# A two-block-plus-one transformer kernel: score matmuls a block ahead, maxima ahead of the scaling, weighted values ahead of the transposes, constant products at the head of attention units

## The chip, the cores and the metric

One core of one Trainium2 chip runs the whole program in one launch. The metric is the device time in microseconds (us). The tensor engine (TensorE, PE in the rows), the vector engine (VectorE, DVE), the scalar engine (ScalarE, ACT), GpSimd (POOL) and the DMA queues (SP among them) each run their own instruction list in order and meet by semaphores.

## The reference

Three layers follow each other on 1024 tokens of width 1024. The change concerns their attention parts:

```python
# layer 1: 8 heads of 64, chunks of 64 queries see their own and the 8 chunks before
scores = einsum('bcqhd,bckhd->bhcqk', qc, kb) * Dh ** -0.5 + bias   # masked: -1e30
probs = softmax(scores, axis=-1)
out = einsum('bhcqk,bckhd->bcqhd', probs, vb)
# layer 2: 8 query heads on 2 key heads, window of 128 to both sides, with a sink
mx = maximum(s.max(-1), sk); e = exp(s - mx)
prob = e / (e.sum(-1) + exp(sk - mx))
# layer 3: attention of 8 heads to a neighbourhood of 8 rows x 16 columns of a grid,
# relative bias, gated by silu(z); beside it a depthwise convolution of 31 taps
```

Everything else (projections, spatial gating, mLSTM scan, feed-forward parts, norms) is computed by both versions in the same way.

## The kernel before

Activations lie feature-major. Every weight block (128 x 1024) is split by GpSimd into a high and a low part (lines 2046 and 2060), and TensorE makes three products per tile (`product`, `block_part`: line 389, 407). These fill most of the time.

Attention is done for two heads at a time (a "unit"): four units in layer 1 (buffers `band_...`, keys of 128, 256, 384, 512 and then four times 640 for the eight blocks of 128 queries), four in layer 2 (`local_...`, called with `joint=True`, 256 or 384 keys) and four in layer 3 (`near_...`, 512 or 576 keys). In a unit the eight query blocks p = 0 to 7 go through the same steps:

- S(p), `score`: the scores of both heads on TensorE, into the two accumulators `acc[0]` and `acc[1]`, one a head (line 709; in layer 2 both heads share one accumulator, line 697). It first waits until both accumulators are free.
- `take_scores(p)` on VectorE (line 813, in layer 2 line 777) adds the bias, writes the negated scores and their minimum, and frees the accumulators.
- `exponential(p)` on ScalarE (line 854, 846), with the sum of the row.
- `norm_probs(p)` on VectorE: reciprocal of the sum (line 823, 789) and scaling (line 826, 793).
- T(p), `turn_probs`: TensorE transposes the probabilities in tiles of 128 (line 720) into three PSUM banks `turned`, and `copy_turned(p)` on ScalarE copies them to SBUF (lines 864, 870).
- W(p), `weigh_values`: TensorE multiplies them by the values (line 744).

The order on each engine is written out by hand. TensorE runs, for n = 0 to 9: S(n), T(n-1), W(n-2) (layer 2: S(n+1), T(n-1), W(n-2)). At n = 8 and 9 it also runs pieces of the next weight block (three tiles ahead of T(7), one ahead of W(7)), which cover the last waits. VectorE runs `norm_probs(p-1)` and then `take_scores(p)`; in layer 2 the other way round. ScalarE runs `exponential(n)` and then `copy_turned(n-1)`, in all layers and in both versions.

In layer 3 the scores are exponentiated in place (`scores=None`). VectorE has the taps of the convolution to do between the units there (line 1733) and adds finished rows to `h` (line 897).

`keep_clock(pe, n)` (line 502) issues n products of constants, 128 x 128 by 128 columns, whose result nobody reads (line 504). It stands at norms and a few other places. The units of layer 1 run as a loop of two turns with two units each, with waits on register values (`t.loop`).

Of the kernel before, what the change touches and what calls it, by code (L numbers as in the profile page):

```python
# [155 lines left out]
def mixer_program(nc, x_t, blocks, n_blocks, params, consts, bias_1, bias_2, bias_3, sgu_rows, sgu_w, p_t,  # L156
                  out_t):

    with ExitStack() as ctx:
# [23 lines left out]
        def attention_buffers(base, kib, probs_kib, bias_kib, bias_width):  # L183
# [76 lines left out]

        near = Buffers(
            q_t=at("near_q_t", 140.625, [P, TOK]), k_t=at("near_k_t", 144.625, [P, TOK]),
            v_tok=at("near_v_tok", 148.625, [P, TT, P]), v_t=at("near_v_t", 156.625, [P, TOK]), scores=None,
            probs=at("near_probs", 152.625, [P, 2, 2, 640]), probs_t=at("near_probs_t", 162.625, [P, 2, 2, 5, P]),
            total=at("near_att_sum", 172.625, [P, TOK]), bias=None)
        near_bias = at("near_bias", 188.625, [P, 2, 2, 576])
# [413 lines left out]

        def att_tensor(pe, t, a, keys, next_block=True, joint=False):

            ahead = 1 if joint else 0

            def rows_of(side):
                return slice(64 * side, 64 * side + 64)
# [25 lines left out]
            def turn_probs(p):  # L714

                count = keys(p)[1]

                def turn(bank, side, c, at):
                    w = min(P, count - c * P)
                    return pe.transpose(turned[bank][0:w, at * P:(at + 1) * P],  # L720
                                        a.probs[:, p % 2, side, ahead + c * P:ahead + c * P + w], ident[:, :])
# [12 lines left out]

            def weigh_values(p):
                first, count, _ = keys(p)
                tiles = -(-count // P)
                if p == TT - 1:
                    for _ in range(3 if count > HALF else 2):
                        pe.wait_ge(turned_copied, t.next("turned_copied"))  # L740
                for c in range(tiles):
                    w = min(P, count - c * P)
                    for side in range(2):
                        ins = pe.matmul(att_out[rows_of(side), p % 4 * P:(p % 4 + 1) * P],  # L744
                                        a.v_tok[0:w, first // P + c, rows_of(side)],
                                        a.probs_t[0:w, p % 2, side, c, :], start=(c == 0), stop=(c == tiles - 1))
                if p % 4 == 3:
                    ins.then_inc(pv_done, 1)

            for n in range(ahead):  # L750
                score(n)
            for n in range(TT + 2):
                if n + ahead < TT:
                    score(n + ahead)
                if n == TT and next_block:
                    slot, s = take_block(pe, t), claim(pe, t)
                    take_turn(pe, t)
                    block_part(pe, t, slot, s, 0, 3)
                if 1 <= n <= TT:
                    turn_probs(n - 1)  # L760
                if n >= 2:
                    if n == TT + 1 and next_block:
                        block_part(pe, t, slot, s, 3, 4)
                    weigh_values(n - 2)
            if next_block:
                block_part(pe, t, slot, s, 4, KT)

        def window_vector_steps(dve, t, ch, a, keys, n):
# [15 lines left out]

            def norm_probs(p):
                count, own = keys(p)[1], 8 * (p % 2)
                for side in range(2):
                    dve.wait_ge(exp_done, t.next("exp_done"))
                    ch.link(dve.reciprocal(small[:, own + 4 + side:own + 5 + side],
                                           small[:, own + 2 + side:own + 3 + side]))  # L790
                    ch.sync()
# [10 lines left out]
        def att_vector(dve, t, ch, a, keys, bias_of=None):  # L802
            def take_scores(p):
                _, count, bias_at = keys(p)
                if bias_of is None:
# [4 lines left out]
                ch.link(dve.memset(small[:, 60:61], 3e38))  # L810
                ch.sync()
                for side, s in enumerate(slots):
                    dve.tensor_tensor_reduce(
                        out=a.probs[:, p % 2, side, 0:count] if a.scores is None else a.scores[:, side, 0:count],
                        in0=acc[s][:, 0:count], in1=table[:, side, :], scale=-1.0,
                        scalar=small[:, 60:61], op0=ALU.add, op1=ALU.min,
                        accum_out=small[:, side:side + 1]).then_inc(acc_free[s], 1)

            def norm_probs(p):
                count = keys(p)[1]  # L820
                for side in range(2):
                    dve.wait_ge(exp_done, t.next("exp_done"))
                    ch.link(dve.reciprocal(small[:, 4 + side:5 + side], small[:, 2 + side:3 + side]))
                    ch.sync()
                    probs = a.probs[:, p % 2, side, 0:count]
                    dve.tensor_scalar(probs, probs, small[:, 4 + side:5 + side], None, ALU.mult).then_inc(p_ready, 1)

            for p in range(TT + 1):
                if p >= 1:
                    norm_probs(p - 1)  # L830
                if p < TT:
                    take_scores(p)

        def att_scalar(act, t, ch, a, keys, joint=False, bias=None, load_bias=None):

            def exponential(p, side):
                count = keys(p)[1]
                if joint:
# [3 lines left out]
                    else:  # L842
# [10 lines left out]
                probs = a.probs[:, p % 2, side, 0:count]  # L853
                act.activation(probs, probs if a.scores is None else a.scores[:, side, 0:count], ACT.Exp,
                               scale=-1.0, bias=small[:, side:side + 1],
                               accum_out=small[:, 2 + side:3 + side]).then_inc(exp_done, 1)

            def copy_turned(p):

# [56 lines left out]

        def att1_tensor(pe, t):
            feature_pair(pe, t, expect_parts(t, KT))
            with t.loop(2, acc0=20, acc1=20, block=6, p_ready=32, turned_copied=40, hi_ready=2, lo_ready=2):
                for _ in range(2):  # L920
                    projections_tensor(pe, t)
                    att_tensor(pe, t, band, keys_1)
                    feature_block(pe, t)
                    t.next("hi_ready")
                    t.next("lo_ready")

        def att1_scalar(act, t, ch):
            ch.reset()
            with t.loop(2, acc0=20, acc1=20, turned_full=40, pv_done=4, hi_ready=2, lo_ready=2) as i:
                for q in range(2):  # L930
                    act.dma_start(band.bias[:, :, :], bias_1[bass.ds(2 * i + q, 1)].rearrange("a p s k -> p (a s) k"))\
                        .then_inc(bias_in, 16)
                    qkv_scalar(act, t, band)
                    att_scalar(act, t, ch, band, keys_1)
                    split_hi(act, t, band.total[:, :],
                             att_hi[:, bass.ds(2 * i + q, 1), :].rearrange("p a n -> p (a n)"))
                    t.next("lo_ready")
                ch.reset()

        def att1_vector(dve, t, ch):  # L940
            ch.reset()
            with t.loop(2, acc0=20, acc1=20, exp_done=32, bias_in=2, hi_ready=2, lo_ready=2) as i:
                for q in range(2):
                    pass_acc(t, 4)
                    dve.wait_ge(bias_in, t.next("bias_in") * 16)
                    att_vector(dve, t, ch, band, keys_1)
                    where = bass.ds(2 * i + q, 1)
                    split_lo(dve, t, band.total[:, :], att_hi[:, where, :].rearrange("p a n -> p (a n)"),
                             att_lo[:, where, :].rearrange("p a n -> p (a n)"))
                ch.reset()  # L950

# [823 lines left out]
        def near_tensor(pe, t):  # L1775
            feature_block(pe, t)
            for n in range(HEAD_PAIRS):
# [572 lines left out]
```

## Time and profile before

| | |
|---|---|
| median of 3 runs | 3624.6 us (3622.15 to 3625.77) |
| the profiled execution, its own time | 3623.64 us |
| its span, first to last instruction | 3621.9 us |
| TensorE busy | 96% of the span |
| VectorE, ScalarE, GpSimd busy | 48%, 22%, 33% |
| mean granted TensorE clock | 0.985 |

The span is what the rows below divide up; 1.7 us of the profiled execution lie around it. Busy shares are means over stages with different limits, so each attention unit is read by itself. Rows of the weight loads (PEld) show best where TensorE waits, because the modelled ends of matmuls run into waits. A granted clock of 1.00 is 2.4 GHz and 0.50 is 1.2 GHz.

### The profile page before, as it was taken

Reading aid. Unit: us, or ns where it says so; the run is one execution under the profiler, and the core shown is the slowest. Engines: PE = TensorE matmul, PEld = TensorE weight load, DVE = VectorE, ACT = ScalarE, POOL = GpSimd, SP = SyncE. Lnnn points to the kernel's source line nnn. Section 1 sums busy time; section 2 is a strip of 40 time slices with the busy share of each in tenths; the row PEclk is TensorE's granted clock in tenths of the full one; section 3 lists DMA queues with packets and bytes.
Section 4 is the critical chain, followed back from the end, with each engine's and each line's share of the span. In section 5 each row is a group of like instructions: output and inputs, shape, how many; then the busy total and the mean of one; then the engine's idle time right before and its main releaser. Section 6 shows DMA issues by size and latency. Waiting matters only on the chain.

```text
span 3621.9 us, 41941 instructions
## 1 busy us (share of the span) xinstructions
PE 3478.8 (96%) x16940; PEld 2772.5 (77%) x16940; DVE 1728.9 (48%) x2073; ACT 797.4 (22%) x1170; POOL 1201.0 (33%) x534
## 2 busy tenths in 40 slices
PE   7999999989999999989999999999999999999997
PEld 5767877778888888777876678888888868767675
DVE  4323433352323223588866642322322368888835
ACT  4433100020000000332234430000000141333452
POOL 2222344323433433333321134334333424222222
PEclk9999999999999999999999999999999999999998
DMA  2111211111111111122111011111111101111111
GB/s 95 39 36 38 93 47 46 47 35 47 46 52 46 46 52 46 35 66 81 59 34 33 23 41 47 52 46 46 52 46 58 47 18 60 59 60 58 44 35 64
DMA packets 52163, 178.96 MB, mean 49 GB/s; under 512 B 5728, under 2 KB 6368, under 8 KB 52064
## 3 DMA queue, kind: packets, MB, share of 16 engines
q1 hardware_dynamic: 38016, 138.43, 11.7%
q10 hardware_dynamic: 14048, 39.10, 3.2%
q8 instruction: 75, 1.23, 0.1%
q14 instruction: 24, 0.20, 0.0%
HBM read 172.79 MB, written 4.72 MB: 49 GB/s over the span
## 4 chain that ended last, share of the span: by engine, by line
PE 85%; DVE 8%; ACT 3%; issue 3%; POOL 1%; DMA 0%; ACTq 0%; DVEq 0%; POOLq 0%
PE acc L389 69%; PE acc L407 4%; PE acc L744 2%; PE acc L720 2%; PE acc L709 2%; PE acc L426 2%; DVE conv_slots L1733 1%; PE acc L473 1%; DVE rstd L618 1%; DVE normed L650 1%; DVE x_lo L488 0%; DVE h L897 0%; POOL w_lo L2060 0%; DVE window_scores L777 0%; PE acc L1355 0%
## 5 line engine op out<-in xcount | busy, mean ns | idle before, releaser
L2046 POOL TENSOR_TENSOR w_hi<-raw,zero 128x1024 fp32r<-128x1024 f32 x264 | 515.6, 1953 | 2365.2 <-PE acc L389 1663.1
L389 PE MATMUL acc<-x_hi,w_hi 128*128 128x512 f32 x2512 | 778.4, 391 | 5.7 <-POOL w_lo L2060 3.0
L389 PE MATMUL acc<-x_lo,w_hi 128*128 128x512 f32 x2512 | 774.2, 389 | 0.0
L389 PE MATMUL acc<-x_hi,w_lo 128*128 128x512 f32 x2512 | 774.0, 389 | 0.0
L2060 POOL TENSOR_TENSOR w_lo<-raw,w_hi 128x1024 fp32r<-128x1024 f32 x262 | 678.9, 2591 | 20.5
L897 DVE TENSOR_TENSOR h<-h,acc 128x1024 f32<-128x1024 f32 x312 | 380.7, 1221 | 554.9 <-PE acc L389 554.9
L389 PEld LDWEIGHTS acc<-x_hi,w_hi 128*128 128x128 f32 x2512 | 470.0, 188 | 106.7 <-POOL w_lo L2060 4.7
L389 PEld LDWEIGHTS acc<-x_lo,w_hi 128*128 128x128 f32 x2512 | 471.9, 188 | 98.7
L389 PEld LDWEIGHTS acc<-x_hi,w_lo 128*128 128x128 f32 x2512 | 471.8, 188 | 98.5
L1164 DVE TENSOR_TENSOR hid<-act_g,acc 128x1024 f32<-128x1024 f32 x44 | 53.7, 1221 | 570.7 <-PE acc L389 554.7
L483 ACT ACTIVATE hid_hi<-hid 128x1024 fp32r<-128x1024 f32 x44 | 46.7, 1061 | 909.2 <-DVE hid L1164 909.2
L1733 DVE SCALAR_TENSOR_TENSOR conv_slots<-conv_slots,par 128x1024 f32<-128x1024 f32 x120 | 227.8, 1898 | 4.1
L389 PE MATMUL acc<-hid_hi,w_hi 128*128 128x512 f32 x704 | 217.0, 389 | 0.7 <-DVE hid_lo L488 0.7
L389 PE MATMUL acc<-hid_lo,w_hi 128*128 128x512 f32 x704 | 216.7, 389 | 0.0
L389 PE MATMUL acc<-hid_hi,w_lo 128*128 128x512 f32 x704 | 216.7, 389 | 0.0
L488 DVE TENSOR_TENSOR hid_lo<-hid,hid_hi 128x1024 fp32r<-128x1024 f32 x44 | 138.2, 3140 | 49.9 <-ACT hid_hi L483 49.9
L389 PEld LDWEIGHTS acc<-hid_hi,w_hi 128*128 128x128 f32 x704 | 131.9, 188 | 28.5 <-DVE hid_lo L488 1.1
L389 PEld LDWEIGHTS acc<-hid_lo,w_hi 128*128 128x128 f32 x704 | 132.1, 188 | 27.5
L389 PEld LDWEIGHTS acc<-hid_hi,w_lo 128*128 128x128 f32 x704 | 132.1, 188 | 27.4
L1140 ACT ACTIVATE act_g<-acc 128x1024 f32<-128x1024 f32 x44 | 45.3, 1029 | 360.2 <-PE acc L389 360.1
L504 PEld LDWEIGHTS acc<-ident,mean_w 128*128 128x128 f32 x812 | 95.0, 194 | 21.0 <-issue 20.2
L504 PE MATMUL acc<-ident,mean_w 128*128 128x128 f32 x812 | 95.5, 278 | 16.2 <-DMA h<-x_t 16.2
(332 smaller groups left out, 4068.9 us busy)
## 6 DMA issues: line engine op xcount, KB each, us to landing
raw<-blocks SPq DMA_DIRECT2D x264, 512.0 KB, 3.4
near_bias<-bias ACTq DMA_DIRECT2D x16, 512.0 KB, 4.0
h<-x_t ACTq DMA_DIRECT2D x8, 512.0 KB, 8.2
h<-x_t ACTq DMA_DIRECT2D x1, 4096.0 KB, 15.5
q_past<-q_dram ACTq DMA_DIRECT2D x8, 512.0 KB, 5.6
w_own<-r_dram ACTq DMA_DIRECT2D x8, 512.0 KB, 6.5
out_t<-out_rows ACTq DMA_DIRECT2D x8, 512.0 KB, 3.0
band_bias<-bias ACTq DMA_DIRECT2D x4, 640.0 KB, 4.1
```

Of the source, the lines that this page charges most:

```text
L389: ins = pe.matmul(acc[s][:, c], w[:, slot, tile, :], part[:, c], start=(n == 0 and m == 0), stop=(n == last and m == 2))
L407: ins = pe.matmul(acc[s][:, c], w[:, slot, k, :], part[:, k, c], start=(k == 0 and m == 0), stop=(k == KT - 1 and m == 2))
L426: ins = pe.matmul(acc[accs[b]][:, c], w[:, slots[b], k, :], part[:, k, c], start=(k == 0 and m == 0), stop=(k == KT - 1 and m == 2))
L488: dve.tensor_tensor(lo, source, hi.bitcast(F32), ALU.subtract).then_inc(lo_ready, 1)
L504: pe.matmul(acc_all[:, 2 * TOK:2 * TOK + P], mean_w[:, :], ident[:, :], start=True, stop=True)
L709: ins = pe.matmul(acc[slots[side]][:, c0:c1], a.q_t[rows_of(side), p * P:(p + 1) * P], a.k_t[rows_of(side), first + c0:first + c1], start= ...
L720: return pe.transpose(turned[bank][0:w, at * P:(at + 1) * P], a.probs[:, p % 2, side, ahead + c * P:ahead + c * P + w], ident[:, :])
L744: ins = pe.matmul(att_out[rows_of(side), p % 4 * P:(p % 4 + 1) * P], a.v_tok[0:w, first // P + c, rows_of(side)], a.probs_t[0:w, p % 2, si ...
L897: dve.tensor_tensor(h[:, j, :], h[:, j, :], acc[s], ALU.add).then_inc(acc_free[s], 1)
L1733: ins = dve.scalar_tensor_tensor(out=out, in0=shifted, scalar=weight, in1=out, op0=ALU.mult, op1=ALU.add)
L2046: pool.tensor_tensor(hi, whole, nothing, ALU.add).then_inc(hi_split, 1)
L2060: pool.tensor_tensor(lo, whole, hi.bitcast(F32), ALU.subtract).then_inc(w_split, 1)
```

## The change

- TensorE's order in a unit becomes S(0), then for n = 0 to 9: S(n+1), W(n-2), T(n-1). In layer 2, where S was ahead already, only T and W change places. The waits for copied tiles, which stood before the transposes, now stand before W.
- VectorE takes the scores of block p before it normalizes block p-1 in layers 1 and 3 too. The two reciprocals of a block become one instruction over two columns, which waits for both exponentials, in all layers. The constant 3e38 is set once per unit and not once per block.
- Layer 3 gets a scores buffer of its own. In layers 1 and 3 `take_scores(p)` waits for each head's exponential of p-1, which reads that buffer. The row statistics alternate between two sets of columns.
- Constant products are added: in each unit of layer 1 twelve ahead of the wait for the projections, nine behind S(0), three behind S(1); in each unit of layer 3 ten, eighteen and twelve at the same places.
- The loop over layer 1's units is written out.

```diff
-            v_tok=..., v_t=at("near_v_t", 156.625, [P, TOK]), scores=None,
+            v_tok=..., v_t=at("near_v_t", 156.625, [P, TOK]),
+            scores=at("near_scores", 176.625, [P, 2, 576]),
...
-                    for _ in range(0 if p == 0 else 2 if side and keys(p - 1)[1] > HALF else 1):
-                        pe.wait_ge(turned_copied, t.next("turned_copied"))
...
-                if p == TT - 1:
-                    for _ in range(3 if count > HALF else 2):
-                        pe.wait_ge(turned_copied, t.next("turned_copied"))
+                for _ in range(3 if count > HALF else 2):
+                    pe.wait_ge(turned_copied, t.next("turned_copied"))
...
-            for n in range(ahead):
-                score(n)
+            score(0)
+            keep_clock(pe, idle[0])
             for n in range(TT + 2):
-                if n + ahead < TT:
-                    score(n + ahead)
+                if n + 1 < TT:
+                    score(n + 1)
+                if n == 0:
+                    keep_clock(pe, idle[1])
                 if n == TT and next_block:
                     slot, s = take_block(pe, t), claim(pe, t)
                     take_turn(pe, t)
                     block_part(pe, t, slot, s, 0, 3)
-                if 1 <= n <= TT:
-                    turn_probs(n - 1)
                 if n >= 2:
                     if n == TT + 1 and next_block:
                         block_part(pe, t, slot, s, 3, 4)
                     weigh_values(n - 2)
+                if 1 <= n <= TT:
+                    turn_probs(n - 1)
...
+                for _ in range(2):
+                    dve.wait_ge(exp_done, t.next("exp_done"))
+                ch.link(dve.reciprocal(small[:, own + 4:own + 6], small[:, own + 2:own + 4]))
...
+                for side, s in enumerate(slots):
+                    if p:
+                        dve.wait_ge(exp_done, t.next("exp_done"))
+                    dve.tensor_tensor_reduce(
+                        out=a.scores[:, side, 0:count], in0=acc[s][:, 0:count], in1=table[:, side, :], scale=-1.0,
...
             for p in range(TT + 1):
+                if p < TT:
+                    take_scores(p)
                 if p >= 1:
                     norm_probs(p - 1)
-                if p < TT:
-                    take_scores(p)
...
             feature_block(pe, t)
+            keep_clock(pe, 12)
             await_all_taken(pe, t)
...
-                    att_tensor(pe, t, band, keys_1)
+                att_tensor(pe, t, band, keys_1, idle=(9, 3))
...
+                keep_clock(pe, 10)
                 await_all_taken(pe, t)
-                att_tensor(pe, t, near, keys_3)
+                att_tensor(pe, t, near, keys_3, idle=(18, 12))
```

## Rows read from the trace of the kernel before

**Rows 1.** The page, parts 1 and 4: busy time by engine; the chain that ended last.
```profile
PE 3478.8 (96%) x16940; PEld 2772.5 (77%) x16940; DVE 1728.9 (48%) x2073; ACT 797.4 (22%) x1170; POOL 1201.0 (33%) x534
...
PE 85%; DVE 8%; ACT 3%; issue 3%; POOL 1%; DMA 0%; ACTq 0%; DVEq 0%; POOLq 0%
```

**Rows 2.** Waits of PE, whole span: waiter, releaser, total us, times, longest us.
```profile
PE acc L709 <- DVE small L813: 15.7, 21, 1.8
PE acc L389 <- DVE h L897: 11.8, 5, 4.1
...
PE acc L720 <- DVE local_probs L793: 4.1, 8, 0.7
...
PE acc L720 <- ACT local_probs_t L864: 3.1, 8, 0.5
```

**Rows 3.** Timeline of PEld, layer 1, unit 1: start, us, what, [idle before].
```profile
72.38 0.33 PEld L709 LDWEIGHTS acc<-band_k_t,band_q_t 64*128 64x128 f32 x4 [1.60 <-ACT band_k_t L914]
...
106.53 1.07 PEld L744 LDWEIGHTS acc<-band_probs_t,band_v_tok 128*64 128x64 f32 x20 [0.36 <-issue]
```

**Rows 4.** Timeline of PEld, layer 1, unit 4.
```profile
267.93 0.33 PEld L709 LDWEIGHTS acc<-band_k_t,band_q_t 64*128 64x128 f32 x4 [1.60 <-ACT band_k_t L914]
269.35 0.30 PEld L709 LDWEIGHTS acc<-band_k_t,band_q_t 64*128 64x128 f32 x4 [1.09 <-DVE small L813]
...
288.02 1.07 PEld L744 LDWEIGHTS acc<-band_probs_t,band_v_tok 128*64 128x64 f32 x20 [0.17 <-issue]
289.27 0.30 PEld L709 LDWEIGHTS acc<-band_k_t,band_q_t 64*128 64x128 f32 x4 [0.17 <-issue]
...
290.55 1.08 PEld L720 LDWEIGHTS acc<-ident,band_probs 128*128 128x128 f32 x10
291.79 1.07 PEld L744 LDWEIGHTS acc<-band_probs_t,band_v_tok 128*64 128x64 f32 x20 [0.17 <-issue]
...
301.26 1.07 PEld L744 LDWEIGHTS acc<-band_probs_t,band_v_tok 128*64 128x64 f32 x20 [0.36 <-issue]
```

**Rows 5.** Timeline of PEld, layer 3, units 2 and 3.
```profile
3218.05 0.33 PEld L709 LDWEIGHTS acc<-near_k_t,near_q_t 64*128 64x128 f32 x4 [1.81 <-DVE h L897]
3221.03 0.45 PEld L709 LDWEIGHTS acc<-near_k_t,near_q_t 64*128 64x128 f32 x4 [2.64 <-DVE small L813]
...
3255.42 0.85 PEld L744 LDWEIGHTS acc<-near_probs_t,near_v_tok 128*64 128x64 f32 x16 [0.36 <-issue]
...
3311.36 0.33 PEld L709 LDWEIGHTS acc<-near_k_t,near_q_t 64*128 64x128 f32 x4 [1.82 <-issue]
...
3349.62 0.85 PEld L744 LDWEIGHTS acc<-near_probs_t,near_v_tok 128*64 128x64 f32 x16 [0.36 <-issue]
```

**Rows 6.** Timeline, constant products at the first norm; block products ahead of unit 3.
```profile
27.16 6.86 PE L504 MATMUL acc<-ident,mean_w 128*128 128x128 f32 x60
...
200.73 0.41 PEld L389 LDWEIGHTS acc<-x_lo,w_hi 128*128 128x128 f32 x2
...
201.18 0.41 PEld L389 LDWEIGHTS acc<-x_hi,w_lo 128*128 128x128 f32 x2
```

**Rows 7.** Windows: busy PE, PEld, DVE, ACT, POOL, granted clock, DMA share, GB/s.
```profile
70.00:80.00 10.00, 7.33 (x30) 3.67 (x30) 5.31 (x26) 4.75 (x16) 0.00 (x0) 0.70 0.01 2
...
270.00:280.00 10.00, 8.89 (x52) 4.68 (x50) 8.21 (x32) 5.53 (x18) 0.00 (x0) 0.83 0.00 0
```

**Rows 8.** Timeline of DVE and ACT, one block of 640 keys, layer 1.
```profile
92.44 0.88 DVE L813 CUSTOM_DVE_ANT_0 band_scores<-acc,band_bias,small 128x640 f32<-128x640 f32 x1
...
93.39 0.82 ACT L854 ACTIVATE band_probs<-band_scores,small 128x640 f32<-128x640 f32 x1
...
94.20 1.06 ACT L864 ACTIVATE band_probs_t<-acc 128x512 f32<-128x512 f32 x2
...
94.53 0.55 DVE L826 TENSOR_SCALAR band_probs<-band_probs,small 128x640 f32<-128x640 f32 x1
95.16 0.38 ACT L870 ACTIVATE band_probs_t<-acc 128x256 f32<-128x256 f32 x1
```

More of the change, by code:

```diff
@@ L262, in mixer_program @@
             q_t=at("near_q_t", 140.625, [P, TOK]), k_t=at("near_k_t", 144.625, [P, TOK]),
-            v_tok=at("near_v_tok", 148.625, [P, TT, P]), v_t=at("near_v_t", 156.625, [P, TOK]), scores=None,
+            v_tok=at("near_v_tok", 148.625, [P, TT, P]), v_t=at("near_v_t", 156.625, [P, TOK]),
+            scores=at("near_scores", 176.625, [P, 2, 576]),
             probs=at("near_probs", 152.625, [P, 2, 2, 640]), probs_t=at("near_probs_t", 162.625, [P, 2, 2, 5, P]),
@@ L678, in await_parts, with att_tensor @@
             pe.wait_ge(lo_ready, t.count("lo_ready"))
-        def att_tensor(pe, t, a, keys, next_block=True, joint=False):
-            ahead = 1 if joint else 0
+        def att_tensor(pe, t, a, keys, next_block=True, joint=False, idle=(0, 0)):
+            sink = 1 if joint else 0
             def rows_of(side):
@@ L786, in norm_probs @@
                 count, own = keys(p)[1], 8 * (p % 2)
+                for _ in range(2):
+                    dve.wait_ge(exp_done, t.next("exp_done"))
+                ch.link(dve.reciprocal(small[:, own + 4:own + 6], small[:, own + 2:own + 4]))
+                ch.sync()
                 for side in range(2):
[L788 to L791, printed above, removed]
                     probs = a.probs[:, p % 2, side, 1:1 + count]
@@ L804, in take_scores @@
                 _, count, bias_at = keys(p)
+                own = 8 * (p % 2)
                 if bias_of is None:
@@ L809, in take_scores @@
                 slots = [await_acc(dve, t) for _ in range(2)]
-                ch.link(dve.memset(small[:, 60:61], 3e38))
-                ch.sync()
[L812 to L817, printed above, removed]
@@ L819, in norm_probs @@
-            def norm_probs(p):
-                count = keys(p)[1]
+                for side, s in enumerate(slots):
[3 more added lines that the diff above has]
+                        out=a.scores[:, side, 0:count], in0=acc[s][:, 0:count], in1=table[:, side, :], scale=-1.0,
+                        scalar=small[:, 60:61], op0=ALU.add, op1=ALU.min,
+                        accum_out=small[:, own + side:own + side + 1]).then_inc(acc_free[s], 1)
@@ L821, in norm_probs @@
+            def norm_probs(p):
+                count, own = keys(p)[1], 8 * (p % 2)
+                if p == TT - 1:
+                    for _ in range(2):
+                        dve.wait_ge(exp_done, t.next("exp_done"))
+                ch.link(dve.reciprocal(small[:, own + 4:own + 6], small[:, own + 2:own + 4]))
+                ch.sync()
                 for side in range(2):
-                    dve.wait_ge(exp_done, t.next("exp_done"))
-                    ch.link(dve.reciprocal(small[:, 4 + side:5 + side], small[:, 2 + side:3 + side]))
@@ L824, in norm_probs @@
-                    ch.sync()
                     probs = a.probs[:, p % 2, side, 0:count]
-                    dve.tensor_scalar(probs, probs, small[:, 4 + side:5 + side], None, ALU.mult).then_inc(p_ready, 1)
+                    dve.tensor_scalar(probs, probs, small[:, own + 4 + side:own + 5 + side], None, ALU.mult)\
+                       .then_inc(p_ready, 1)
+            ch.link(dve.memset(small[:, 60:61], 3e38))
+            ch.sync()
             for p in range(TT + 1):
+                if p < TT:
+                    take_scores(p)
@@ L852, in exponential @@
                 act.wait_ge(acc_free[s], t.count(f"acc{s}"))
[L853 to L856, printed above, removed]
+                own = 8 * (p % 2)
+                act.activation(a.probs[:, p % 2, side, 0:count], a.scores[:, side, 0:count], ACT.Exp,
+                               scale=-1.0, bias=small[:, own + side:own + side + 1],
+                               accum_out=small[:, own + 2 + side:own + 3 + side]).then_inc(exp_done, 1)
             def copy_turned(p):
@@ L918, in att1_tensor @@
             feature_pair(pe, t, expect_parts(t, KT))
-            with t.loop(2, acc0=20, acc1=20, block=6, p_ready=32, turned_copied=40, hi_ready=2, lo_ready=2):
-                for _ in range(2):
-                    projections_tensor(pe, t)
-                    att_tensor(pe, t, band, keys_1)
-                    feature_block(pe, t)
-                    t.next("hi_ready")
-                    t.next("lo_ready")
+            for _ in range(HEAD_PAIRS):
+                projections_tensor(pe, t)
+                att_tensor(pe, t, band, keys_1, idle=(9, 3))
+                feature_block(pe, t)
+                t.next("hi_ready")
+                t.next("lo_ready")
@@ L927, in att1_scalar @@
         def att1_scalar(act, t, ch):
             ch.reset()
[L929 to L938, printed above, removed]
+            for n in range(HEAD_PAIRS):
+                act.dma_start(band.bias[:, :, :], bias_1[n]).then_inc(bias_in, 16)
+                qkv_scalar(act, t, band)
+                att_scalar(act, t, ch, band, keys_1)
+                split_hi(act, t, band.total[:, :], att_hi[:, n, :])
+                t.next("lo_ready")
@@ L940, in att1_vector @@
         def att1_vector(dve, t, ch):
             ch.reset()
[L942 to L950, printed above, removed]
+            for n in range(HEAD_PAIRS):
+                pass_acc(t, 4)
+                dve.wait_ge(bias_in, t.next("bias_in") * 16)
+                att_vector(dve, t, ch, band, keys_1)
+                split_lo(dve, t, band.total[:, :], att_hi[:, n, :], att_lo[:, n, :])
```

2 lines of the change are left out of this document (1 added, 1 removed).

## The prediction

> **What bounds the kernel now.** I read the page's busy shares and chain first. TensorE is busy 96% of the span, and 85% of the chain that ended last is its work [rows 1]. So what TensorE is given to do more costs its full time, except where it falls into a hole in which TensorE waits, and a wait that goes is a gain of its length. The list of TensorE's waits is next [rows 2]: those of the score matmuls for `take_scores` (15.7 us in 21 places, nearly all in layers 1 and 3) and of layer 2's transposes (4.1 and 3.1 us) are what the change can reach. Then I read each unit from S(0) to W(7) in the timeline of weight loads, where the reader sees how much of a unit is holes.
>
> Layer 1: 34.15 us in unit 1, 33.33 in unit 4 [rows 3, 4]; the four have a mean of 33.7. Layer 3: 37.4 us in unit 2, 38.3 in unit 3 [rows 5]; mean of four 37.8. TensorE's own work in a unit comes from pitches. In steps of 640 keys S takes 1.28 us (289.27 to 290.55), T 1.24 (to 291.79) and W 1.25 (288.02 to 289.27) [rows 4]; that includes a hole of 0.17 us at each change of kind. A 512-column block product takes 0.227 us (two in 0.45) [rows 6], so four tiles of the next block take 24 x 0.227 = 5.4 us. For fewer keys S, T and W shrink in proportion. Sums: 27.9 us in layer 1 and 32.2 in layer 3. What is left is holes and half clock: 5.8 us and 5.6 us a unit. Ahead of S(0) there is another hole: 1.60 us idle in layer 1 [rows 4] and 1.81 in layer 3 (1.69 in its first unit) [rows 5]; the last block product still streams for 0.23 of it, so 1.37 and about 1.56 us are free. In total the holes of these eight units are 4 x (5.8 + 1.37 + 5.6 + 1.56) = 57 us.
>
> **The change, part by part.**
>
> *Constant products.* 60 of their records took 6.86 us [rows 6]; a product is two records, so one costs 0.229 us. Layer 1 gets 12 + 9 + 3 = 24 a unit, layer 3 10 + 18 + 12 = 40, over four units each 256 products or 58.5 us, all on the bounding engine. That is as much as all the holes above, and not all holes are where the products stand. Nothing waits ahead of them, so they start at once and are never dropped when the awaited data is early.
> Head: twelve take 2.74 us for 1.37 free: +1.37 a unit. Ten take 2.29 for 1.56: +0.73. These two are near certain, since the products are in order ahead of S(0).
> Behind S(0) in layer 3: S(1) stood 2.98 us after S(0) [rows 5]; now it is 1.06 (S of 512 keys) + 18 x 0.229 = 5.2 us after it. In layer 1 it stood at 1.42 [rows 4]; now 0.42 + 9 x 0.229 = 2.5.
>
> *Order on TensorE and VectorE.* I step through the new order by hand. S(n+1) can start when S(n)'s scores are taken. For 128 keys this round took 1.42 us (S(0) to S(1) in layer 1), for 512 keys 2.98 (layer 3); the line through both gives 1.9, 2.5 and 3.5 for 256, 384 and 640, less 0.1 for the memset that goes. Layer 1, S(1) to S(7) then start at 2.5, 4.3, 6.7, 9.5, 12.8, 16.1, 19.6 us after S(0). TensorE waits 0.5, 1.1, 0.8, 0.6 and 0.2 us ahead of S(2) to S(6); from there it has 3.77 us of work a step against a round of 3.4 and waits no more. VectorE has 2 x 0.81 + 0.2 + 2 x 0.55 = 2.9 us a step and ScalarE 2 x 0.81 + 1.06 + 0.38 = 3.1 [rows 8]: neither becomes the bound. The new wait of `take_scores(p)` for the exponentials of p-1 holds back the reciprocal and scaling behind it in VectorE's list, and S behind those on TensorE; ScalarE's list is exponential(n), copy(n-1), exponential(n+1), so T(n-1) to S(n+3) becomes a chain of about 0.7 + 1.06 + 0.38 + 2 x 0.82 + 0.95 = 4.7 us, plus 0.3 for signals. TensorE's own path between the two is 1.24 + 3.77 = 5.0. It costs nothing by that, with no reserve.
> W(5) now follows T(5) with no S between them. Its copies end about 0.7 + 1.06 + 0.38 + 0.1 = 2.2 us after T(5) starts, and T(5) takes 1.24: a new wait of 0.9 us. Behind it stand T(6) and the next weight block. W(6) and W(7) have block tiles ahead of them (4.1 and 1.36 us), which cover their copies.
> So layer 1's W(7) comes at 27.9 + 12 x 0.229 + 4.1 = 34.7 us. Layer 3: S(2) at 9.0, S(3) at 12.0 after 0.85 us of waiting, no further wait but the 0.9 at W(5): W(7) at 32.2 + 30 x 0.229 + 1.7 = 40.8. The same stepping of the old order gives 33.8 and 37.7, so it can be trusted to some tenths. Differences: +0.9 and +3.1 us a unit.
>
> *Half clock.* Ten us at the start of unit 1 had a mean granted clock of 0.70, in unit 4 of 0.83 [rows 7]: 6.0 against 3.4 us at 1.2 GHz, each after the holes around S(0). Unit 1 took 0.8 us more. If the new products keep the clock at 2.4 GHz, a unit gets back some 0.7 us (nothing to 1.7). That leaves +0.2 and +2.4.
> The Trainium skill (TensorE: Matmul & The Clock Gate, What's actually happening) says in effect that the gate halves the clock of an engine that was idle and restores it only after sustained work. By it the products would return all of these stretches, and my sum takes that; without it the sum would be 8 x 0.7 = 5.6 us higher.
>
> *Layer 2.* Only T and W change places. In full steps TensorE has hardly a hole but those of 0.17, so nothing changes there. At both ends of a unit it waits (4.1 + 3.1 = 7.2 us in all, 1.8 a unit) [rows 2]; W moved ahead fills part of these, and the last W directly behind its own T pays some back. I take -0.8 a unit, between 0 and -1.8. The single reciprocal saves 0.2 us of VectorE, which TensorE's full steps hide.
>
> *The rest at nothing:* the memset, the statistics columns and the scores buffer are off TensorE; the loop written out removes register waits that show no hole. [...]
>
> **Sum.** Layer 1: 4 x (1.37 + 0.2) = 6.3. Layer 3: 4 x (0.73 + 2.4) = 12.5. Layer 2: -3.2. Together +15.6 us on the profiled execution's own 3623.6 gives 3639.2; the median of the runs is 1.0 above that execution: **3640 us**.
>
> **Rivals.**
> *No measurable change (3620 to 3631).* The products return more than counted, by full clock and by holes that shrink elsewhere. With 1.7 us a unit back from the clock the sum falls by 8, with layer 2 at its limit by 4 more: 3628. For it: the holes and the products are of one size. Against it: half clock accounts for few tenths of the differences between units.
> *Faster, about 3619.* The 0.17 us hole at a change of kind stands at T to W and W to S [rows 4]. The new order has S to W, W to T and T to S. If two of three had no hole, 8 steps x 8 units x 2 x 0.17 = 22 us would go. It decides from 0.08 us a change downward. Against it: both holes are there though W waited for nothing, so they belong to the change of kind. The Trainium skill (TensorEngine Tiling (Array Packing), Key Properties) says that a change of tiling mode drains the engine; by it all three new changes cost the same and this rival falls.
> *Much slower (over 3652).* The chain through ScalarE has no reserve: 0.4 us more in it on five steps of eight units are 16 us, giving 3656. For it: TensorE's path exceeds the chain by nothing. Against it: the chain repeats only every second step.
> *VectorE bounds layer 3.* TensorE waits for finished rows of `h` between some units (line 897, 11.8 us in 5 places in the whole program) [rows 2], behind the convolution. Then a later W(7) is partly hidden and the last scaling counts, which comes some 2.4 us later and not 3.1. It would take 3 us off and leave the forecast's sign: 3637.
>
> **How the numbers follow.** Forecast with its last variant 0.72, own range 3632 to 3650; no change 0.13; faster 0.04; much slower 0.11. A change within 0.2%, 7.2 us, can't be told from none. The low end takes in 1.7 us a unit from the clock; the high end a head of layer 3 without cover and no return of the clock. Range 3628 to 3653. Faster 0.04, same 0.12, slower 0.84.
>
> **What would show it.** Line 504's group grows from 812 records by 512. S(0) of layer 1 starts 1.4 us later behind the last block product, S(1) of layer 3 5.2 us behind S(0). A wait for a copy stands ahead of W(5) in each unit. Full steps of layer 1 last 3.8 us. Units: about 34 (layer 1) and 40 us (layer 3). Layer 3 not over 38 us, or steps over 4.1 us in layer 1, would make the prediction wrong, the one way or the other.

## The result, and the profile after

The kernel after takes **3647.8 us** (median of four runs, 3646.6 to 3650.6) against 3623.4 on the same chip: a ratio of 1.007, 95% interval 1.0055 to 1.0085. It is slower, as forecast, and 7.8 us above the 3640 forecast. The span of the profiled execution grew from 3621.9 to 3645.3 us.

The page after, parts 1 and 4, answering to [rows 1]; then the waits of TensorE (engine line waited for, total us, times, longest us), answering to [rows 2]:

```profile
PE 3510.6 (96%) x17452; PEld 2824.0 (77%) x17452; DVE 1693.5 (46%) x1921; ACT 798.8 (22%) x1170; POOL 1200.2 (33%) x534
...
PE 87%; DVE 8%; ACT 2%; issue 2%; POOL 1%; DMA 0%; ACTq 0%; DVEq 0%; POOLq 0%
```
```profile
PE acc L710 <- DVE small L814: 16.2, 25, 1.1
PE acc L390 <- DVE h L902: 11.5, 5, 4.1
...
PE acc L742 <- ACT local_probs_t L869: 4.2, 6, 0.7
...
PE acc L742 <- ACT band_probs_t L875: 3.5, 4, 0.9
PE acc L742 <- ACT near_probs_t L875: 3.5, 4, 0.9
...
PE acc L721 <- DVE local_probs L793: 2.8, 4, 0.7
```

TensorE has 512 records and 31.8 us of work more. The wait of the score matmuls is as large as before although the scores go a block ahead: 16.2 us in 25 places against 15.7 in 21. Two waits are new, those for the copies of `turned` ahead of W(5), once in each unit of layers 1 and 3. In layer 2 the waits for the scaling and for the copies sum to 7.0 us where they were 7.2. VectorE has 35 us less work, and TensorE's waits for it are no shorter by that.

One unit of layer 1 (unit 4) and one of layer 3 (unit 2) in the timeline of weight loads (start, us, what, [idle before]), answering to [rows 4] and [rows 5]; L505 are the constant products:

```profile
275.97 2.88 PEld L505 LDWEIGHTS acc<-ident,mean_w 128*128 128x128 f32 x24
278.97 0.30 PEld L710 LDWEIGHTS acc<-band_k_t,band_q_t 64*128 64x128 f32 x4
279.39 2.08 PEld L505 LDWEIGHTS acc<-ident,mean_w 128*128 128x128 f32 x18
281.60 0.30 PEld L710 LDWEIGHTS acc<-band_k_t,band_q_t 64*128 64x128 f32 x4
...
298.94 0.30 PEld L710 LDWEIGHTS acc<-band_k_t,band_q_t 64*128 64x128 f32 x4 [0.17 <-issue]
...
300.22 1.07 PEld L742 LDWEIGHTS acc<-band_probs_t,band_v_tok 128*64 128x64 f32 x20
301.47 1.07 PEld L721 LDWEIGHTS acc<-ident,band_probs 128*128 128x128 f32 x10 [0.17 <-issue]
303.64 1.10 PEld L742 LDWEIGHTS acc<-band_probs_t,band_v_tok 128*64 128x64 f32 x20 [1.10 <-ACT band_probs_t L875]
...
314.15 1.07 PEld L742 LDWEIGHTS acc<-band_probs_t,band_v_tok 128*64 128x64 f32 x20 [0.35 <-issue]
...
3228.60 2.43 PEld L505 LDWEIGHTS acc<-ident,mean_w 128*128 128x128 f32 x20
3231.15 0.30 PEld L710 LDWEIGHTS acc<-near_k_t,near_q_t 64*128 64x128 f32 x4
3232.21 4.09 PEld L505 LDWEIGHTS acc<-ident,mean_w 128*128 128x128 f32 x36 [0.76 <-issue]
3236.42 0.30 PEld L710 LDWEIGHTS acc<-near_k_t,near_q_t 64*128 64x128 f32 x4
...
3272.75 0.85 PEld L742 LDWEIGHTS acc<-near_probs_t,near_v_tok 128*64 128x64 f32 x16 [0.35 <-issue]
```

From the first S to the start of the last W it is 314.15 - 278.97 = 35.2 us where it was 33.3, and 3272.75 - 3231.15 = 41.6 where it was 37.4. Below I give a unit from S(0) to the end of the last W, as the mean of the layer's four (one W, about 1 us, longer than those):

| kernel | layer 1 | layer 3 | layer 2, units 1 to 4 |
|---|---|---|---|
| before | 34.75 | 38.63 | 26.77, 27.44, 27.45, 21.77 |
| after | 36.35 | 42.31 | 25.83, 26.43, 26.43, 22.41 |

Following how far S(0) and the last W have moved gives where the 23.4 us came from: 12.9 in layer 1 (6.4 in the bodies of four units, 1.44 ahead of S(0) in units 2 to 4 and 2.20 in the first); -1.6 between it and layer 2; -2.3 in layer 2; -0.6 up to layer 3; 17.0 in layer 3 (14.7 in the bodies, 0.75 at each of three heads; the fourth lies ahead of this stretch); -2.0 behind it.

The granted clock came back. Windows over the attention units of layer 1 and of layer 3 with what lies between them, before and after (window, length, busy us of PE, PEld, DVE, ACT, POOL, granted clock, DMA share, GB/s):

```profile
60.00:340.00 280.00, 263.76 (x1611) 197.64 (x1612) 96.16 (x292) 106.33 (x240) 60.52 (x28) 0.96 0.12 38
3100.00:3500.00 400.00, 380.10 (x2136) 279.42 (x2135) 305.52 (x415) 167.66 (x285) 110.67 (x42) 0.97 0.17 53
```
```profile
60.00:340.00 280.00, 262.70 (x1751) 207.48 (x1750) 78.72 (x231) 107.42 (x240) 56.00 (x27) 1.00 0.11 35
3100.00:3500.00 400.00, 387.44 (x2378) 296.76 (x2377) 282.43 (x349) 153.73 (x272) 102.13 (x39) 1.00 0.18 51
```

A mean of 0.96 is 2 x 0.04 of the time at 0.50. So before spent some 2 x 0.04 x 280 + 2 x 0.03 x 400 = 46 us of these windows at 1.2 GHz (an estimate from rounded means); after, next to none.

### The profile page after: what moved, and what is told of

Its sections match the earlier page's. It is cut to its first block, busy times and chain, and to the rows that moved or that the text cites. A ratio compares the mean times of both kernels' runs of the same rounds, so it can differ in the third digit from the quotient of the medians.

```text
span 3645.3 us, 42445 instructions
## 1 busy us (share of the span) xinstructions
PE 3510.6 (96%) x17452; PEld 2824.0 (77%) x17452; DVE 1693.5 (46%) x1921; ACT 798.8 (22%) x1170; POOL 1200.2 (33%) x534
## 3 DMA queue, kind: packets, MB, share of 16 engines
q1 hardware_dynamic: 38016, 138.43, 12.2%
## 4 chain that ended last, share of the span: by engine, by line
PE 87%; DVE 8%; ACT 2%; issue 2%; POOL 1%; DMA 0%; ACTq 0%; DVEq 0%; POOLq 0%
PE acc L390 69%; PE acc L408 4%; PE acc L742 2%; PE acc L710 2%; PE acc L721 2%; PE acc L505 2%; PE acc L427 1%; DVE conv_slots L1730 1%; PE acc L474 1%; DVE rstd L619 1%; DVE band_scores L814 1%; DVE normed L651 1%; PE acc L698 0%; DVE x_lo L489 0%; POOL w_lo L2058 0%
## 5 line engine op out<-in xcount | busy, mean ns | idle before, releaser
L505 PEld LDWEIGHTS acc<-ident,mean_w 128*128 128x128 f32 x1324 | 155.1, 194 | 29.8 <-issue 27.9
L505 PE MATMUL acc<-ident,mean_w 128*128 128x128 f32 x1324 | 158.6, 278 | 16.5 <-DMA h<-x_t 16.5
```

Of the source, the lines that this page charges most:

```text
L505: pe.matmul(acc_all[:, 2 * TOK:2 * TOK + P], mean_w[:, :], ident[:, :], start=True, stop=True)
```

## The experiments

The forecast's theory: the products cost more than the holes they fill, the order costs the wait at W(5) and little else, and layer 2 gains. Its rivals: the order alone is the loss, the products alone are, or the clock they hold decides. The first four kernels take the change apart, the next four act on one cost each, and the last two are made from what these showed. In none of them is a result left out; the products' sums are read by nobody.

**The new order without the products.**

```
-            keep_clock(pe, 12)
...
-                att_tensor(pe, t, band, keys_1, idle=(9, 3))
+                att_tensor(pe, t, band, keys_1, idle=(0, 0))
...
-                keep_clock(pe, 10)
...
-                att_tensor(pe, t, near, keys_3, idle=(18, 12))
+                att_tensor(pe, t, near, keys_3, idle=(0, 0))
```

> The changed kernel with all 256 added constant products of layers 1 and 3 left out; order, buffers and the rest as changed. Theory A (the products are plain TensorE work, more than the holes they stand in, and the clock returns nothing): heads give back 1.4 us in layer 1 and 0.75 in layer 3, bodies 1.1 and 3.3 us a unit, together 26 us: about 3621 us against 3647.8, with S(0) to the last W 35.1 us in layer 1 and 38.9 in layer 3. Theory B (the products keep the clock up and this is worth its time): half clock comes back at the head of units and costs 0.7 to 1.7 us in each of eight units, so 3627 to 3636 us.

Measured 3639.0 us (five runs), ratio 1.0044 (1.003 to 1.0058). Units 37.86 and 40.66 us: in layer 1 they are longer *without* products than with (36.35), in layer 3 shorter (42.31). The weight loads at its first unit of layer 1, and its windows:

```profile
73.26 0.33 PEld L710 LDWEIGHTS acc<-band_k_t,band_q_t 64*128 64x128 f32 x4 [1.60 <-ACT band_k_t L919]
74.72 0.37 PEld L710 LDWEIGHTS acc<-band_k_t,band_q_t 64*128 64x128 f32 x4 [1.13 <-DVE small L814]
76.95 0.53 PEld L710 LDWEIGHTS acc<-band_k_t,band_q_t 64*128 64x128 f32 x4 [1.87 <-DVE small L814]
```
```profile
60.00:340.00 280.00, 254.49 (x1558) 189.85 (x1557) 78.71 (x231) 107.70 (x240) 56.12 (x27) 0.93 0.11 35
3100.00:3500.00 400.00, 372.70 (x2109) 275.48 (x2108) 287.22 (x353) 163.09 (x280) 109.26 (x42) 0.97 0.17 51
```

The same four loads take 0.53 us instead of 0.33: half clock (0.50 from 76.9 to 78.6 us), after holes of 1.1 and 1.9 us. The order alone costs 15.7 us, and in layer 1 it meets more half clock than before did (0.93 against 0.96). The last experiment runs the same order at next to full clock, with units of 35.15 and 38.99 us: of the units here, 2.7 and 1.7 us go with the half clock.

**Without the products at the heads alone.**

```
-            keep_clock(pe, 12)
...
-                keep_clock(pe, 10)
```

> The changed kernel without the twelve and the ten constant products ahead of the wait for the projections; those behind S(0) and S(1) stay. Theory A: S(0) of each unit starts 1.4 us (layer 1) and 0.75 us (layer 3) earlier behind the last block product, bodies as before: 8.7 us less than the changed kernel, about 3639 us. Theory B: half clock comes in units whose head has no products, and some of the products behind S(0) run at 1.2 GHz: no gain, 3645 to 3652 us.

Measured 3639.6 us (four runs), ratio 1.0047 (1.0031 to 1.0062). That is 8.3 us less than after; units stay at 36.38 and 42.35 and both windows at 1.00. So the heads are a pure cost, of the forecast's size (4 x 1.37 + 4 x 0.73 = 8.4): the granted clock is 1.00 without them too.

**The products in the old order.**

```
+            keep_clock(pe, 12)
...
+                keep_clock(pe, 10)
...
+                if n < 2:
+                    keep_clock(pe, idle[n])
```
(with `idle` of (9, 3) and (18, 12), as in the kernel after; the loop over layer 1's units stays)

> The kernel before with nothing changed but the 256 constant products, at the same places. Theory A: the products alone cost 1.4 + 1.3 us a unit in layer 1 and 0.75 + 3.6 in layer 3, 28 us, so 3651 us, or 3646 if all of the half clock is returned. Rival C (the loss is in the new order): this kernel stays within 10 us of the kernel before, under 3634 us.

Measured 3639.8 us (four runs), ratio 1.0047 (1.0031 to 1.0062). Units 34.68 and 41.35: nothing in layer 1 (before 34.75), +2.7 in layer 3. So order and products, each alone, cost 16 us, and together 24.

**T ahead of W again, with the scores still a block ahead.**

```
+                if 1 <= n <= TT:
+                    turn_probs(n - 1)
                 if 2 <= n <= TT + 1:
                     weigh_values(n - 2)
-                if 1 <= n <= TT:
-                    turn_probs(n - 1)
```
(the waits for copied tiles go back ahead of the transposes)

> The changed kernel with the transposes ahead of the weighted values again in each step (as in the kernel before, in all layers), everything else as changed. If the new order of T and W is what costs: the waits ahead of W (0.9 us at W(5), 1.1 in two records of layer 3) go and layer 2 loses its gain of 2.3 us; stepping gives 0.3 us less in a unit of layer 1 and 0.7 in layer 3, so 4 us less in these and 2.3 more in layer 2: about 3646 us. If the order of T and W is what helps, it is over 3652 us.

Measured 3657.6 us (four runs), ratio 1.0097 (1.0081 to 1.0112): 9.8 us worse than after. Units 37.27 and 42.95, longer by 0.9 and 0.6; layer 2's units are back at 26.69, 27.27, 27.31 and 21.47. It keeps the single reciprocal, so that alone is worth 0.1 to 0.3 us in a unit of layer 2. The wait moves from the copies to the scaling: TensorE then waits 4.6 us in 4 places of layer 1 for `band_probs`. With the scores ahead, W ahead of T is the better of the two in the sum of each layer; only layer 2's last unit is quicker without it. The units explain some 8 of the 9.8 us; where the rest lies wasn't followed.

**Layer 2's new order alone, on the kernel before.**

```
-                if 1 <= n <= TT:
+                if 1 <= n <= TT and not joint:
                     turn_probs(n - 1)
                 if 2 <= n <= TT + 1:
                     weigh_values(n - 2)
+                if 1 <= n <= TT and joint:
+                    turn_probs(n - 1)
```
(with the waits for copied tiles ahead of W and the single reciprocal, in layer 2 alone)

> The kernel before with layer 2's part of the change alone: weighted values ahead of the transposes, one reciprocal for both heads. If parts add up as the S(0) times say (three units of 26.4 for 27.3 us and one of 22.4 for 21.8), 2.3 us less than the kernel before, 3620 us, too small to be told in the time but plain in the unit lengths. Rival: the reciprocal alone brings it (VectorE bound), then the transposes no longer wait for VectorE and the first to third unit shrink by over 1.5 us each.

Measured 3619.0 us (eleven runs), ratio 0.999 (0.9981 to 0.9999): a gain of 3 to 4 us, of which 2.4 lie in layer 2's units. They take 25.78, 26.46, 26.41 and 22.41: 1.0 less in the three that have a next block, 0.6 more in the one that has none, as in the kernel after. The rival, that the reciprocal brings it, fell with the experiment above. A full step from S to S, in the kernel before and then in the kernel after:

```profile
1885.52 0.30 PEld L697 LDWEIGHTS acc<-conv_in,local_queries 64*128 64x128 f32 x4 [0.17 <-issue]
...
1887.98 0.30 PEld L697 LDWEIGHTS acc<-conv_in,local_queries 64*128 64x128 f32 x4 [0.17 <-issue]
```
```profile
1896.10 0.30 PEld L698 LDWEIGHTS acc<-conv_in,local_queries 64*128 64x128 f32 x4 [0.17 <-issue]
1896.95 0.64 PEld L742 LDWEIGHTS acc<-local_probs_t,local_v_tok 128*64 128x64 f32 x12 [0.55 <-ACT local_probs_t L869]
1897.76 0.64 PEld L721 LDWEIGHTS acc<-ident,local_probs 128*128 128x128 f32 x6 [0.17 <-issue]
1898.56 0.30 PEld L698 LDWEIGHTS acc<-conv_in,local_queries 64*128 64x128 f32 x4 [0.17 <-issue]
```

Both steps take 2.46 us. The new one's holes are at S to W (shown as 0.55, most of it S itself still streaming), W to T and T to S (0.17 each). The full step is no shorter by the new order.

**The old order with fewer products**, only as many as the holes hold: 5 ahead of a unit of layer 1 and 6 ahead of one of layer 3, and behind S(0) and S(1) 4 and 1 in layer 1, 7 and 4 in layer 3.

```
-            keep_clock(pe, 12)
+            keep_clock(pe, 5)
-                    att_tensor(pe, t, band, keys_1, idle=(9, 3))
+                    att_tensor(pe, t, band, keys_1, idle=(4, 1))
...
-                keep_clock(pe, 10)
+                keep_clock(pe, 6)
-                att_tensor(pe, t, near, keys_3, idle=(18, 12))
+                att_tensor(pe, t, near, keys_3, idle=(7, 4))
```

> The kernel before with constant products cut to the holes they stand in: 5 and 6 at the heads, 4 and 1 behind S(0) and S(1) in layer 1, 7 and 4 in layer 3, 88 in all. If half clock costs about 1 us a unit in the old order (the full 256 products left layer 1's units at 34.7 us, as without them), the units of both layers shrink by 0.7 to 1.5 us and the kernel takes 3612 to 3618 us. Rival: the smaller number doesn't hold the clock, units stay at 34.7 and 38.6 us and the kernel at 3623.

(Its count of 88 is a slip: they are 4 x 10 + 4 x 17 = 108, and TensorE has 216 records more than before.) Measured 3611.2 us (five runs), ratio 0.9965 (0.9952 to 0.9979): **some 12 us faster than before**. Units 33.69 and 37.44 where before had 34.75 and 38.63. Its windows, and the weight loads of its unit 2 of layer 3:

```profile
60.00:340.00 280.00, 270.40 (x1713) 207.56 (x1712) 95.68 (x292) 107.36 (x241) 61.38 (x29) 1.00 0.12 38
3100.00:3500.00 400.00, 392.83 (x2292) 295.42 (x2291) 301.16 (x413) 170.64 (x287) 110.99 (x43) 1.00 0.18 54
```
```profile
3212.82 0.33 PEld L709 LDWEIGHTS acc<-near_k_t,near_q_t 64*128 64x128 f32 x4 [0.23 <-DVE h L899]
3213.91 1.64 PEld L504 LDWEIGHTS acc<-ident,mean_w 128*128 128x128 f32 x14 [0.76 <-issue]
3215.80 0.33 PEld L709 LDWEIGHTS acc<-near_k_t,near_q_t 64*128 64x128 f32 x4 [0.25 <-issue]
```

S(1) stands 2.98 us behind S(0), exactly as before [rows 5]: seven products fit in the hole, and S is not late. The clock stays at 1.00. The products return 1.06 us in a unit of layer 1 and 1.19 in one of layer 3, 4 x 2.25 = 9 us in these eight units; that is what half clock had cost there.

**The first tile of the next block ahead of W(5)**, on the kernel after.

```
-                if n == TT and next_block:
+                if n == TT - 1 and next_block:
...
-                    block_part(pe, t, slot, s, 0, 3)
+                    block_part(pe, t, slot, s, 0, 1)
+                if n == TT and next_block:
+                    block_part(pe, t, slot, s, 1, 3)
```

> The changed kernel with one of the three tiles of the next weight block moved from ahead of W(6) to ahead of W(5), between T(5) and W(5), in all layers. If the 1.1 us idle ahead of W(5) is a wait for the copies and nothing else, 1.36 us of useful work hides it: each unit of layers 1 and 3 is 1.1 us shorter, those of layer 2 that have a next block 0.8: 11 us less than the changed kernel, about 3637. Rival: the wait turns up again ahead of T(6), whose scaling waits behind exponential(7) in ScalarE's list, and under 4 us are gained.

Measured 3639.2 us (four runs), ratio 1.0046 (1.003 to 1.0061): 8.6 us less than after. Its unit 4 of layer 1:

```profile
299.58 1.07 PEld L721 LDWEIGHTS acc<-ident,band_probs 128*128 128x128 f32 x10 [0.17 <-issue]
300.62 0.30 PEld L408 LDWEIGHTS acc<-x_hi,w_hi 128*128 128x128 f32 x2
...
302.21 1.07 PEld L742 LDWEIGHTS acc<-band_probs_t,band_v_tok 128*64 128x64 f32 x20 [0.36 <-issue]
```

The wait for `band_probs_t` is gone. Units are 0.9 us shorter in layers 1 and 3, layer 2's first three 0.75. The wait at W(5) is real and costs its length.

**VectorE in its old order** (the scaling of p-1 ahead of the scores of p), on the kernel after.

```
+                if p:
+                    norm_probs(p - 1)
                 if p < TT:
                     take_scores(p)
-                if p:
-                    norm_probs(p - 1)
```
(the waits of `take_scores` for the exponentials go back into `norm_probs`)

> The changed kernel with VectorE's list in the old order in layers 1 and 3 (scaling of p-1 ahead of the scores of p); TensorE's order and the products as changed. The round from S(n) to S(n+2) then holds the exponential and the scaling too: about 4.6 us for 640 keys where it was 3.4, over TensorE's 3.8 a step. If the round of the scores sets a unit, each unit grows by 3 to 5 us, 3670 to 3690. If TensorE's work sets it, the time stays within 5 us of 3648.

Measured 3670.7 us (four runs), ratio 1.0134 (1.0118 to 1.0149): 22.9 us worse. Units 39.09 and 45.16. The waits of TensorE in 60 to 340 us; the kernel after has 12.2 us in 20 places there:

```profile
PE acc L710 <- DVE small L812: 22.8, 24, 1.4
```

With the scores a block ahead, VectorE's round is what S waits for, so taking the scores ahead of the scaling is a part that the new order can't do without.

**All that gained, in one kernel**: old order and 108 products in layers 1 and 3; in layer 2 W ahead of T, where a next block follows, with its first tile ahead of W(5); one reciprocal.

```
-                if 1 <= n <= TT:
+                if 1 <= n <= TT and not (joint and next_block):
...
+                if 1 <= n <= TT and joint and next_block:
+                    turn_probs(n - 1)
```
(beside the edits of the products, the reciprocal and the tile shown above)

> The kernel before with what paid in the runs so far: constant products cut to their holes (5 and 6 at heads, 4 and 1, 7 and 4 behind S(0) and S(1)), and in layer 2 one reciprocal, the new order of weighted values and transposes in the three units with a next block, and one tile of that block ahead of W(5). If the parts add: -11 us of the products, -2.9 us of the order (three units of 26.4 for 27.3) and three times 0.8 of the tile, so 3605 to 3608 us. If the layers interact, over 3611.

Measured **3606.3 us** (five runs, 3602.8 to 3606.6), ratio 0.9952 (0.9938 to 0.9965). Units 33.70 and 37.44, layer 2's 24.98, 25.69, 25.69 and 21.49. It is the fastest here, 17 us under before and 42 under after.

**The new order with those 108 products.**

```
-            keep_clock(pe, 12)
+            keep_clock(pe, 5)
...
-                att_tensor(pe, t, near, keys_3, idle=(18, 12))
+                att_tensor(pe, t, near, keys_3, idle=(7, 4))
```

> The changed kernel with its constant products cut to 5 and 6, 4 and 1, 7 and 4. Theory D (the new order has holes of its own, in the first steps and ahead of W(5), that no clock explains): S(0) to the last W 35.3 us in layer 1 and 39.5 in layer 3 against 33.7 and 37.4 with the same products in the old order, so about 3625 us. Theory E (the new order is as good as the old one once the clock is held and the products are cut): 33.7 and 37.4 us and 3609 us.

Measured 3621.5 us (ten runs), ratio 0.9995 (0.9986 to 1.0004): as fast as before, 26.3 us under after, and 10.4 above the same products in the old order. Units 2 and 3 of layer 1 take 35.15 (1 and 4 took 35.60 and 35.96, with some half clock in this window), layer 3's 38.99.

```profile
60.00:340.00 280.00, 261.50 (x1678) 203.68 (x1679) 78.69 (x231) 107.78 (x240) 59.97 (x28) 0.99 0.12 37
```

Against the old order with the same products and the same clock, a unit is 1.5 us longer in each layer. Where, the two timelines show: first the old order (unit 4), then the new (unit 3).

```profile
265.67 0.33 PEld L709 LDWEIGHTS acc<-band_k_t,band_q_t 64*128 64x128 f32 x4 [0.25 <-ACT band_k_t L917]
...
286.29 0.30 PEld L709 LDWEIGHTS acc<-band_k_t,band_q_t 64*128 64x128 f32 x4 [0.17 <-issue]
...
287.57 1.07 PEld L720 LDWEIGHTS acc<-ident,band_probs 128*128 128x128 f32 x10
...
298.30 1.07 PEld L744 LDWEIGHTS acc<-band_probs_t,band_v_tok 128*64 128x64 f32 x20 [0.36 <-issue]
```
```profile
203.79 0.33 PEld L710 LDWEIGHTS acc<-band_k_t,band_q_t 64*128 64x128 f32 x4 [0.25 <-ACT band_k_t L920]
...
207.21 0.33 PEld L710 LDWEIGHTS acc<-band_k_t,band_q_t 64*128 64x128 f32 x4 [0.96 <-DVE small L814]
...
209.58 0.33 PEld L710 LDWEIGHTS acc<-band_k_t,band_q_t 64*128 64x128 f32 x4 [1.29 <-DVE small L814]
...
222.67 0.30 PEld L710 LDWEIGHTS acc<-band_k_t,band_q_t 64*128 64x128 f32 x4 [0.17 <-issue]
...
227.36 1.10 PEld L742 LDWEIGHTS acc<-band_probs_t,band_v_tok 128*64 128x64 f32 x20 [1.10 <-ACT band_probs_t L875]
...
237.87 1.07 PEld L742 LDWEIGHTS acc<-band_probs_t,band_v_tok 128*64 128x64 f32 x20 [0.35 <-issue]
```

S(7) comes 20.62 us after S(0) in the old order and 18.88 in the new: the scores are ahead by 1.74 us. But at S(7) the new order still owes a T and a W of a full step more, 1.24 + 1.25 = 2.49 us. So up to S(7) it has lost 0.75 us in holes, net of those of the old order (S(2) and S(3) wait 0.96 and 1.29 us). From S(7) to the last W it takes 15.20 us and the old order 12.01: 3.19, of which 2.49 is that work and the other 0.70 holes, the 1.10 at W(5) above all. 0.75 + 0.70 = 1.45 us a unit.

## Why the prediction was right in its direction, and where its size was off

**Products: right.** The group of `mean_w` weight loads went from 812 to 1324 records, +512 as forecast:

```profile
L505 PEld LDWEIGHTS acc<-ident,mean_w x1324: 186/192/333, 16.5 to 3625.3; 128*128 128x128 f32 x190
```

The heads cost 1.44 and 0.75 us (1.37 and 0.73), and 2.20 in the first unit. S(1) stands 281.60 - 278.97 = 2.63 us behind S(0) (2.5) and in layer 3 5.27 (5.2). The products that fit in no hole are the largest part of the loss: 26.3 us lie between after and the same order with 108 of them.

**The wait at W(5): right**, 1.10 us on the weight loads and 0.9 on the matmuls (0.9); moving a tile in front took 8.6 us off in the whole program. **Full steps of layer 1: right**, 298.94 to 301.47 + 1.24 = 302.71 is 3.77 us (3.8). The new chain through ScalarE cost nothing in them.

**Layer 2: -2.3 us (-3.2).** The three units with a next block gained 0.9 to 1.0 each, the one without paid 0.6; the sum had 0.8 for all four.

**The failed term: a unit's new length, +0.2 and +2.4 us, was +1.6 and +3.7.** That is 4 x (1.4 + 1.3) = 10.8 us, more than the whole error of 7.8. The step that failed is the sentence "The same stepping of the old order gives 33.8 and 37.7, so it can be trusted to some tenths", and the clock's credit behind it. The stepping holds no half clock, and the units it was compared with do. At a clock of 1.00 and with products only in the holes, the old order takes 298.30 - 265.67 = 32.6 us in layer 1 and 36.6 in layer 3: the stepping is 1.2 and 1.1 us too long for the old order. For the new one, with its full products, it gave 34.7 and 40.8 and the trace shows means of 35.3 and 41.5: 0.6 and 0.7 too short. The agreement with the kernel before came from two errors that cancelled: what the stepping had too much stood for the half clock in the measured units. Then 0.7 a unit was credited for the clock coming back, a second time. That is 5.6 of the 10.8 us. The other 5.2 are the new order's stepping: it put S(7) 19.6 us behind S(0), the trace has 298.94 - 278.97 = 19.97, and the rest is spread over the waits behind it. By luck they are nearly made up by the 4.2 us that went between and behind the layers, which the forecast didn't have. Without the credit it would have been 3640 + 5.6 = 3646, beside the measured 3648, and that closeness too would have rested on this luck. The Trainium skill (TensorE: Matmul & The Clock Gate, What's actually happening) was used for its direction, that steady work keeps the clock up, and the windows above agree (0.96 and 0.97 to 1.00). The mistake was in what the credit was subtracted from.

**The rivals.** *No change* needed 1.7 us a unit back from the clock; the clock gave back 1.06 and 1.19 in the old order. The new order with 108 products takes the time of the kernel before (0.9995), but that is another change. *Faster*, by holes that vanish at changes of kind, fell: a full step takes 3.77 us in layer 1 and 2.46 in layer 2 in both orders. The Trainium skill (TensorEngine Tiling (Array Packing), Key Properties) says that the engine drains when the tiling mode changes; the rows agree as far as they go: 0.17 us at W to T and at T to S, and none from T to a block tile of the same 128 x 128 form (299.58 + 1.07 and 300.62 above). Behind S the loads of layer 1 show no hole in either order, and no run isolates the drain. *Much slower* fell with the full step of 3.77 us. *VectorE bounds layer 3*: the wait for `h` is 11.5 us in 5 places (11.8 before), and layer 3 came out above its forecast (3.7 us a unit in place of 2.4), not 3 us below.

**Open.** Between and behind the layers after is 1.6, 0.6 and 2.0 us quicker than before; no run was made to find out why, nor why the first head costs 2.20 us. No run has the loop over layer 1's units written out alone. With 108 products S(0) of unit 3 stands 65.47 us behind S(0) of unit 2 in the new order and 63.99 in the old one, with its loop: the difference of 1.48 is that of the unit itself, so the loop shows no cost and no gain there. That the order meets more half clock than before is read from the windows of the kernel without products; what decides it wasn't isolated. A difference that its rows show is the hole ahead of S(2): 1.87 us at a stretch, where the old order has T(0) between two holes of 0.63 and 0.84 us.

## What to carry to other kernels

Filling an engine's holes to hold its clock paid here up to the length of the holes and not beyond: 108 products won 12 us, and 256 in the same order lost 16. Scores a block ahead can win only what holes the full steps have, and every unit pays for the depth at both ends; here eight short steps with hardly a hole in the full ones left nothing to win, and 1.5 us a unit to pay. Check a hand-made stepping on units that have the same clock as it assumes; agreement with units at another clock can be two errors that cancel.

## What the runs showed of the hardware

- Some 46 us at 1.2 GHz cost about 9 us in the old order. Four score matmuls of 384 columns last 1.65 us at a granted clock of 0.50 (the kernel without products, at 76.98) and 0.92 at full clock (layer 2), close to twice. So 46 us of nothing but work would have cost about 20 us (an estimate); the rest of it must have been waiting, or work that was done before what TensorE waited for next.
- With 10 products a unit in layer 1 and 17 in layer 3 the old order ran at a granted clock of 1.00. In the new order the same products left layer 1 at 0.99.
- W to T and T to S show 0.17 us on the weight loads, even where nothing is awaited, as T to W and W to S did before. The order of the three kinds leaves the length of a full step as it was.
